# Gated delta rule and memory attention on Trainium2: every engine's queue order written out anew

## The reference, cut to what matters

```python
def gated_delta_rule(q, k, v, a, b, a_log, dt_bias):
    ...
    kk = jnp.einsum("bhnid,bhnjd->bhnij", kc, kc)
    lower = jnp.where(strict, bc[..., :, None] * kk * decay, 0.0)
    ...
    sol = lax.linalg.triangular_solve(lower + jnp.eye(CHUNK, dtype=f32), rhs, ...)
    p = jnp.einsum("bhnid,bhnjd->bhnij", qc, kc) * decay
    ...
    def step(state, xs):
        v_new = u_n - jnp.einsum("bhcd,bhde->bhce", w_n, state)
        o_n = jnp.einsum("bhcd,bhde->bhce", qg_n, state) + jnp.einsum("bhij,bhje->bhie", p_n, v_new)
        state = state * gl_n[..., None, None] + jnp.einsum("bhcd,bhce->bhde", kg_n, v_new)
        return state, o_n

def memory_attention(q_mem, mem_k, mem_v):
    s = jnp.einsum("bhtd,bhmd->bhtm", q, k).astype(jnp.float32) * MEM_DH ** -0.5
    p = jax.nn.softmax(s, axis=-1).astype(v.dtype)
    return merge_heads(jnp.einsum("bhtm,bhmd->bhtd", p, v))

y_mix, q_mem = gdn_branch(u @ gdn_w_in, ...)      # o = rms_norm(o, out_norm) * silu(z)
y_mem = memory_attention(q_mem, mem_k, mem_v)
y = jnp.concatenate([y_mix, y_mem], axis=-1) @ w_out
```

## Time and profile before

| | us |
|---|---|
| median of 3 runs | 2048.93 |
| lowest and highest | 2047.54, 2051.88 |
| the profiled execution's time | 2042.87 |
| its span | 2040.9 |
| TensorE busy in it | 1943.8 |
| VectorE busy | 1049.4 |
| ScalarE busy | 753.8 |

### The profile page before, as it was taken

How to read it: one execution, slowest core, us unless ns; L and a number is a source line. 1 busy time by engine, 2 the same in 40 slices (tenths; PEclk the granted TensorE clock), 3 DMA queues, 4 the chain that set the end, 5 groups by cost and what they waited for, 6 DMA issues and landing times.

```text
span 2040.9 us, 28553 instructions
## 1 busy us (share of the span) xinstructions
PE 1943.8 (95%) x11408; PEld 1692.7 (83%) x11408; DVE 1049.4 (51%) x1480; ACT 753.8 (37%) x1232; POOL 33.0 (2%) x31
## 2 busy tenths in 40 slices
PE   8999998999999997999999999999787999999997
PEld 8887788999999996888888777777686898888886
DVE  5644374664444458544444666676426253323335
ACT  5354342432232434423223425553445352212222
POOL 0100000100000000000000000000000000000000
PEclk9999999999999998999999999999778999999998
DMA  5211101233222332232223232222001223223221
GB/s 180 65 61 42 55 1 52 83 94 93 92 84 92 93 94 93 83 104 93 92 93 94 79 106 73 73 73 83 1 1 63 93 73 103 94 84 102 94 84 61
DMA packets 46607, 161.87 MB, mean 79 GB/s; under 512 B 4832, under 2 KB 7136, under 8 KB 46368
## 3 DMA queue, kind: packets, MB, share of 16 engines
q1 hardware_dynamic: 46208, 158.60, 24.5%
q10 hardware_dynamic: 288, 1.70, 0.2%
HBM read 156.09 MB, written 4.19 MB: 79 GB/s over the span
## 4 chain that ended last, share of the span: by engine, by line
PE 88%; DVE 6%; ACT 3%; DVEq 1%; issue 1%; DMA 0%; ACTq 0%; SPq 0%
PE ps L446 76%; PE ps L944 2%; PE ps L860 1%; DVE wlo L2126 1%; PE ps L964 1%; PE ps L833 1%; DVE W L2519 1%; PE ps L575 1%; PE ps L831 1%; PE ps L1107 1%; DVE AM L2305 1%; PE ps L1070 0%; PE ps L1104 0%; ACT RR L1960 0%; PE ps L1097 0%
## 5 line engine op out<-in xcount | busy, mean ns | idle before, releaser
L446 PE MATMUL ps<-UH,whi 128*128 128x264 f32 (+2 forms) x1920 | 655.1, 341 | 10.7 <-DVE wlo L2126 9.2
L446 PE MATMUL ps<-UL,whi 128*128 128x264 f32 (+2 forms) x1920 | 646.8, 337 | 0.0
L446 PE MATMUL ps<-UH,wlo 128*128 128x264 f32 (+3 forms) x1632 | 530.8, 325 | 0.0
L1351 ACT ACTIVATE whi<-raw 128x1024 fp32r<-128x1024 f32 x284 | 297.8, 1053 | 444.6 <-PE ps L446 424.8
L446 PEld LDWEIGHTS ps<-UH,whi 128*128 128x128 f32 x1920 | 365.0, 190 | 53.2 <-issue 12.6
L446 PEld LDWEIGHTS ps<-UL,whi 128*128 128x128 f32 x1920 | 364.7, 190 | 40.2 <-issue 2.4
L446 PEld LDWEIGHTS ps<-UH,wlo 128*128 128x128 f32 (+1 forms) x1632 | 309.6, 190 | 25.2
L2126 DVE TENSOR_TENSOR wlo<-raw,whi 128x1024 fp32r<-128x1024 f32 x248 | 308.1, 1245 | 39.7 <-ACT whi L1351 39.5
L446 PE MATMUL ps<-HH,whi 128*128 128x264 f32 (+1 forms) x768 | 246.4, 321 | 0.0
L446 PE MATMUL ps<-HL,whi 128*128 128x264 f32 (+1 forms) x768 | 246.3, 321 | 0.0
L446 PE MATMUL ps<-HH,wlo 128*128 128x264 f32 (+1 forms) x768 | 245.7, 320 | 0.0
(11 more groups left out here) (437 smaller groups left out, 2356.3 us busy)
## 6 DMA issues: line engine op xcount, KB each, us to landing
raw<-W SPq DMA_DIRECT2D x284, 512.0 KB, 3.5
H<-xT SPq DMA_DIRECT2D x4, 528.0 KB, 6.5
spill<-H SPq DMA_DIRECT2D x1, 2048.0 KB, 8.9
H<-spill SPq DMA_DIRECT2D x1, 2048.0 KB, 8.6
MEM<-memT ACTq DMA_DIRECT2D x1, 1024.0 KB, 4.7
out<-H SPq DMA_DIRECT2D x2, 512.0 KB, 2.9
out<-H SPq DMA_DIRECT2D x4, 256.0 KB, 3.1
masks<-masks SPq DMA_DIRECT2D x1, 768.0 KB, 9.9
```

The costliest lines, as they stand in the source:

```text
L446: mm = pe.matmul(dst, a, b, start=start and n == 0, stop=stop_ and n == 2)
L1351: act.activation(whi[s % NB][:, :, :], raw[s % NB][:, :, :], ACT.Copy).then_inc(w_hi, 1)
```

## The change

In the weights' layout, the levels' numbering, the memory map and the last projection tiles:

```diff
+    sizes[TILE0["wout2"]], sizes[TILE0["wout2"] + 1] = 16, 8
...
-LEVEL_ORDER = [(0, 32), (1, 32), (0, 64), (1, 64), (2, 32), (2, 64), (3, 32), (3, 64)]
+LEVEL_ORDER = [(0, 32), (0, 64), (1, 32), (2, 32), (1, 64), (2, 64), (3, 32), (3, 64)]
...
+        am_t, = region(scratch, ("am_t", [P, 2, SEQ], F32))
...
+        TXI, = region(S0 + 36 * SEQ * 4, ("TXI", [P, 32, 32], F32))
...
+                    if j == 34 and k in (2, 6):
+                        scores(k // 4)
...
             def scores(h):
+                b = 4 + 2 * (h % 2)
+                pe.wait_ge(*evacuated(TILE0["gin"] + 32 + h))
+                if h == 0:
+                    pe.wait_ge(N["l2_done"], 16)
+                    pe.wait_ge(G["dec"], 8)
+                if h >= 2:
+                    pe.wait_ge(N["ma_end"], h - 1)
...
+                    mm = pe.matmul(ps[:, b + c // 2, NMEM * (c % 2):NMEM * (c % 2 + 1)],
```

So the first 8 blocks of the output projection are now the memory heads' blocks of tiles 0 and 1, the next 16 the delta heads' blocks of tile 0 and of tile 1. The memory heads' products lie in PSUM banks 4 to 7 by the head's parity. TensorE's order (what was there before, with its loop over c, is removed):

```diff
                 b, p = 2 * (c % 2) if c < 2 else 0, c % 2
+                if c < 2:
+                    pe.wait_ge(G["pt"], 2 * c + 2)
+                else:
+                    pe.wait_ge(G["up"], levels_done(0 if c == 2 else 2, 64))
                 pe.wait_ge(G["base"], c + 1)
-                pe.wait_ge(G["inv"], 2)
...
+                turned(2 if c < 2 else 3, lambda x: YG[g][:, x, :]).then_inc(G["ot"], 1)
+
+            def memory_part(e):
+                t = TILE0["wout2"] + e
+                if e == 0:
+                    pe.wait_ge(N["om_hi"], HEADS)
+                    pe.wait_ge(N["om_lo"], HEADS)
+                for k in range(HEADS):
+                    wh, wl = take()
+                    passes(psum(t, SEQ), wh, wl, oh(k), ol(k), k == 0, False)
+
+            def heads_part(e):
+                t = st.tile
+                assert t == TILE0["wout2"] + e
+                for k in range(HEADS, 12):
+                    if k in (HEADS, 2 * HEADS):
+                        pe.wait_ge(G["lo"], 6 + k // HEADS)
+                    wh, wl = take()
+                    mm = passes(psum(t, SEQ), wh, wl, oh(k), ol(k), False, k == 11)
+                mm.then_inc(tile_done, 1)
+                st.tile += 1
...
-            for e in range(KT - 2):
-                tile(12, SEQ, oh, ol, before=mixed(e))
+            for j in range(36):
+                tile(KT, SEQ, u, ul, before=between(j))
+
+            pe.wait_ge(G["vtc"], 7)
+            queries(0, 1)
+            pe.wait_ge(*evacuated(TILE0["gin"] + 34))
+            queries(1, 0)
+            pe.wait_ge(G["vtc"], 8)
+            queries(2, 3)
+            shares_turned(0)
+            pe.wait_ge(*evacuated(TILE0["gin"] + 35))
+            queries(3, 2)
+            corner32(0)
+            memory_values(0)
+            shares_turned(1)
+            update32(0)
+            scores(2)
+            corner64(0)
+            memory_values(1)
+            corner32(1)
+            update64(0)
+            scores(3)
+            update32(1)
+            corner32(2)
+            shares_turned(2)
+            corner64(1)
+            memory_values(2)
+            update32(2)
+            shares_turned(3)
+            update64(1)
+            memory_values(3)
+            corner64(2)
+            pe.wait_ge(G["up"], levels_done(1, 64))
+            keys_turned(0, 2)
+            solved(0, 0)
+            keys_turned(1, 3)
+            solved(0, 1)
+            outer(0, 0)
+            update64(2)
+            within(0, 0)
+            state_keys(1, 0)
+            outer(0, 1)
+            corner32(3)
+            within(0, 1)
+            pe.wait_ge(G["kg"], 1)
+            keys_turned(2, 2)
+            state_keys(1, 1)
+            solved(1, 0)
+            state_queries(1, 0)
+            outer(1, 0)
+            update32(3)
+            pe.wait_ge(G["kg"], 2)
+            keys_turned(3, 3)
+            within(1, 0)
+            solved(1, 1)
+            state_queries(1, 1)
+            pe.wait_ge(G["kg"], 3)
+            outputs_turned(0, 0)
+            state_keys(2, 0)
+            pe.wait_ge(G["kg"], 4)
+            keys_turned(4, 3)
+            outer(1, 1)
+            within(1, 1)
+            state_queries(2, 0)
+            pe.wait_ge(G["kg"], 5)
+            queries(4, 3)
+            solved(2, 0)
+            pe.wait_ge(G["gt"], 1)
+            outputs_turned(0, 1)
+            state_keys(2, 1)
+            corner64(3)
+            pe.wait_ge(G["pt"], 5)
+            keys_turned(5, 3)
+            outer(2, 0)
+            within(2, 0)
+            state_queries(2, 1)
+            pe.wait_ge(G["gt"], 2)
+            outputs_turned(1, 0)
+            solved(2, 1)
+            pe.wait_ge(G["kg"], 6)
+            queries(5, 3)
+            update64(3)
+            state_keys(3, 0)
+            outer(2, 1)
+            pe.wait_ge(G["pt"], 6)
+            queries(6, 3)
+            within(2, 1)
+            state_queries(3, 0)
+            state_keys(3, 1)
+            pe.wait_ge(G["gt"], 3)
+            outputs_turned(1, 1)
+            solved(3, 0)
+            pe.wait_ge(G["pt"], 7)
+            queries(7, 3)
+            state_queries(3, 1)
+            solved(3, 1)
+            memory_part(0)
+            within(3, 0)
+            within(3, 1)
+            pe.wait_ge(G["pt"], 8)
+            outputs_turned(2, 0)
+            pe.wait_ge(G["gt"], 5)
+            outputs_turned(2, 1)
+            memory_part(1)
+            pe.wait_ge(G["gt"], 6)
+            outputs_turned(3, 0)
+            pe.wait_ge(G["gt"], 7)
+            outputs_turned(3, 1)
+            heads_part(0)
+            heads_part(1)
+            for e in range(2, KT - 2):
+                tile(12, SEQ, oh, ol)
```

ScalarE: the copies of the inverse in projection tile 34, squares into a region of their own, and the order:

```diff
+                if x == 10:
+                    act.wait_ge(G["inv"], 1)
+                    for q in range(4):
+                        a = 32 * q
+                        act.activation(WU[a:a + 32, :, a:a + 32], TXI[a:a + 32, :, :].rearrange("p t n -> p n t"), ACT.Copy)
...
+                    act.activation(squares[:, 4 * g + x, :], QS[g][:, x, :], ACT.Square, accum_out=SS[:, 4 * g + x:4 * g + x + 1])
...
+            wout2 = BLOCK0["wout2"] // SLOT
+            exps(0)
+            exps(1)
+            base(0)
+            shares_out(0)
+            base(1)
+            corner32(0)
+            memory_out(0)
+            shares_out(1)
+            exps(2)
+            corner64(0)
+            memory_out(1)
+            corner32(1)
+            base(2)
+            exps(3)
+            corner32(2)
+            shares_out(2)
+            corner64(1)
+            memory_out(2)
+            shares_out(3)
+            base(3)
+            memory_out(3)
+            keys_out(0, 2)
+            solved(0, 0)
+            corner64(2)
+            keys_out(1, 3)
+            solved(0, 1)
+            weights_hi(0, to=wout2 + 1)
+            for h in range(HEADS):
+                memory_hi(h)
+            rstd_heads(0, 0)
+            corner32(3)
+            keys_out(2, 2)
+            solved(1, 0)
+            queries_out(1, 0)
+            rstd_heads(0, 1)
+            weights_hi(0, to=wout2 + 2)
+            keys_out(3, 3)
+            rstd_heads(1, 0)
+            solved(1, 1)
+            queries_out(1, 1)
+            keys_out(4, 3)
+            gated_hi(0, 0)
+            rstd_heads(1, 1)
+            queries_out(2, 0)
+            solved(2, 0)
+            gated_hi(0, 1)
+            corner64(3)
+            keys_out(5, 3)
+            rstd_heads(2, 0)
+            queries_out(2, 1)
+            solved(2, 1)
+            gated_hi(1, 0)
+            queries_out(3, 0)
+            rstd_heads(2, 1)
+            gated_hi(1, 1)
+            solved(3, 0)
+            queries_out(3, 1)
+            solved(3, 1)
+            rstd_heads(3, 0)
+            gated_hi(2, 0)
+            rstd_heads(3, 1)
+            gated_hi(2, 1)
+            act.wait_ge(G["kv"], 6)
+            weights_hi(0, to=wout2 + 4)
             gated_hi(3, 0)
```

VectorE: the elimination's steps, the transposes, and the order; last the weights' layout on the host:

```diff
-            steps = (0, 2, 4, 6, 8, 11, 14, 17, 20, 23, 27, 31)
...
+            steps = (0, 3, 6, 9, 13, 17, 21, 25, 29, 31)
...
-                else:
+                elif x < len(steps):
                     eliminate(steps[x - 1], steps[x])
...
+                if x == 9:
+                    dve.drain()
+                    dve.transpose(TXI[:, :, :], XI[:, :, :]).then_inc(G["inv"], 1)
+                if x == 10:
+                    dve.transpose(TDG[:, :, :], XI[:, :, :].rearrange("p t s -> p s t")).then_inc(G["inv"], 1)
+                    top(0)
+                    top(1)
...
+            share(0)
+            queries(0, 1)
+            queries(1, 0)
+            share(1)
+            queries(2, 3)
+            queries(3, 2)
+            update32(0)
+            top(2)
+            share(2)
+            update64(0)
+            top(3)
+            update32(1)
+            share(3)
+            update32(2)
+            update64(1)
+            state(0, 0)
+            update64(2)
+            memory_lo(0)
+            output(0, 0)
             dve.drain()
```

(88 more changed lines are left out.)

237 lines of the change are left out of this document (39 added, 198 removed).

## The result

The changed kernel takes **1988.65 us** (median of 4 runs, 1986.23 to 1993.70) against 2048.23 (2047.35 to 2051.88) for the kernel before: ratio 0.9709, 95% interval 0.9684 to 0.9734. The forecast was 2004.7 with a range from 1990 to 2030: the direction was right, the size too small. Its profiled execution took 1990.95 us. The page of that profile answers to the earlier trace rows: the dip of slices 29 to 31 is gone.

The account below looks back on a forecast made before the run. TensorE bounds the kernel, with 35.1 us of waits and clock 0.81 in one stretch; 3.8 + 97.9 + 2 + 5 + 11.2 + 9.5 = 129.4 us against 173.6, gain 44.2, giving 2004.7 us, range 1990 to 2030.

Parts of the forecast that it names:

- part (7): TensorE's clock in the stretch: falls at narrow level-32 updates (5 us) and the idle end (4.5), 9.5 us, bounds 0 and 29.
- rival A: The clock stays full throughout, also at the end: 119.9 us, gain 53.7, 1995 us; chance 0.10.
- (4): New queue orders in the chain: the 35.1 us of waits shrink to 2 us up to the last chunk, bounds 0 and 10.
- (5): The chain's end: memory parts fill one wait, normalize, turn and gate remain, 5 us of TensorE idleness.
- The work: TensorE's products in the new chain, summed from unit prices at full clock: 97.9 us.
- Part (2): VectorE's elimination done by projection tile 33, four steps leaving 0.16 us idle in a tile: cost 0, bounds 0 and 2 us.
- Part (3): Beside tiles 34 and 35, four ScalarE copies of 2.0 us each, ending about 2 us before the chain begins.
- Part (1): Scores of heads 0 and 1 move into projection tile 34: 3.8 us there, winning only an earlier softmax start.
- B: The clock behaves as now though the waits are gone: 29 us in place of 9.5, gain 24.7, 2024 us; chance 0.17.
- C: The queues lock elsewhere and the 35.1 us of waits come back: gain 16, 2033 us; chance 0.11.
- D: The chain, now without rests, runs at 1.2 GHz all through: 222.8 us, loss 49, 2098 us; chance 0.05.
- E: Nothing moves, as the stretch is hidden; chance 0.02.

Follow-up runs that it names:

- e12: The changed kernel run again with nothing edited: 1988.99 us, ratio 0.9722.
- e1: The changed kernel with the level-32 updates of chunks 1 and 2 side by side, no work added: 2002.93 us, ratio 0.9775.
- e2: The changed kernel with chunk 0's level-32 update issued three times, its products left narrow: 2003.64 us, ratio 0.9773.
- e3: The changed kernel with chunk 0's level-32 update issued three times, its products widened to 128 columns: 1999.47 us, ratio 0.976.
- e4: The kernel before, order untouched, with the products of corners and level-32 updates widened to 128 columns: 2031.97 us, ratio 0.9914.
- e5: The changed kernel with the memory heads' products of output tiles 0 and 1 put back behind the last turned outputs: 1995.42 us, ratio 0.975.
- e6: The changed kernel with the scores of memory heads 0 and 1 put back behind the projection: 1992.79 us, ratio 0.9745.
- e10: The changed kernel with two neighbours swapped in ScalarE's and in VectorE's written-out orders: 1994.19 us, ratio 0.9753.
- e13: The two-swaps kernel (e10) run again with nothing edited, on one chip with the changed kernel: 1989.21 us, ratio 0.9721.

## Why the prediction was wrong, and what of it was right

In the terms of its sum, the stretch was forecast at 12.0 (tiles 34 and 35 as before) + 129.4 = 141.4 us, and measured at 129.3: 12.1 us too long.

**The step that failed is part (7), the clock.** It put 9.5 us on it: a fall by the narrow products in the four updates 32 (5), and the fall at the idle end (4.5). The profiled execution has 0.0, the clock is 1.00 throughout; e12 has 3.0, about half of it at each place. The mechanism was right. e1, e2 against e3, and e4 show that narrow products lower the clock of a busy TensorE, and in e12 the two places are the ones forecast: 1488 to 1492 directly behind the single update 32 of chunk 3, with no wait ahead, and 1533 to 1537 at the end. The size was wrong, because I took the price of the first fall from the earlier trace rows, where two updates stand in a row in the middle of other head products, and the fall lasts 11 us. Where one update stands alone the fall is under 4 us long, or doesn't come: in the changed kernel three narrow groups in a row, 5.30 us long, ran at 1.00. The 4.5 us for the end have no working, and the rows of before give less: half of the 1.85 us that TensorE is busy from 1571 to 1577.66, and (1 - 0.89) / 0.5 x 18.91 / 2 = 2.1 us behind, 3.0 together:

```profile
1571.00:1577.66 6.66, 1.85 (x9) 1.49 (x9) 4.06 (x6) 1.66 (x5) 0.00 (x0) 0.54 1.03 407
```

The lower bound of 0 was in the text; rival A (clock full, 119.9 us, or 131.9 with the tiles) had a chance of 0.10 and was the outcome.

**Idleness, parts (4) and (5)**: 2 + 5 us forecast, 5.0 measured (0.9 up to the last chunk, 4.1 at the end, against 1.5 + 1.9 + 1.6). The first place named as tight, the first corner behind the base blocks, is the 0.9 us wait; the others kept their slack. The longest wait is at the end, as forecast. e5 shows that the memory parts cover some of it.

**The work.** 97.9 us forecast for the chain, 97.48 busy from 1431.22 to 1533.72; scores in tile 34, 3.8 forecast, tiles 34 and 35 took 15.29 against 11.99, so 3.3. The heads' part of the output tiles took 11.50 against 11.2. This is 0.6 us too much forecast together, and 9.5 + 2.0 + 0.6 is the 12.1.

**Part (2)**, the elimination in ten tiles, at 0 us: right. From the evacuation of tile 28 to that of tile 33 it took 30.06 us before (1380.90 to 1410.96) and 30.06 after (1385.87 to 1415.93). VectorE waits for TensorE ahead of the evacuations of the fullest tiles, by as little as 0.17 us where 0.16 was forecast.

```profile
1385.87 0.69 DVE L2775 TENSOR_TENSOR ZQ<-ps,R 128x512 f32<-128x512 f32 x1 [0.65 <-PE ps L454]
1391.89 0.69 DVE L2775 TENSOR_TENSOR ZQ<-ps,R 128x512 f32<-128x512 f32 x1 [0.35 <-PE ps L454]
1397.89 0.69 DVE L2775 TENSOR_TENSOR ZQ<-ps,R 128x512 f32<-128x512 f32 x1 [0.17 <-PE ps L454]
```

**Part (3)**, four copies of 2.0 us each: right, 2.07, which end 1.5 us before the chain begins (2 forecast). ScalarE's timeline in tiles 34 and 35:

```profile
1421.38 8.30 ACT L1918 ACTIVATE WU<-TXI 32x1024 f32<-32x1024 f32 x4
1429.69 0.60 ACT L1899 ACTIVATE QKV<-ps 128x512 f32<-128x512 f32 x1
1430.32 0.48 ACT L1931 ACTIVATE am_p<-ps,am_s 128x256 f32<-128x256 f32 x1
```

**Part (1)** said that the early scores win nothing but an earlier softmax; e6 agrees: 0.8 us of waiting.

**The rest of the miss.** The median lies 16.1 us under the forecast: 12.1 of the stretch, 3.3 by which the medians' gain (59.6) exceeds the stretch's (56.3), and 0.7 of the median of before. The 3.3 aren't traced; behind the stretch the two profiled executions take the same time (444.3 and 443.9 us to the end of the span), so they presumably lie ahead of it, where executions spread. Against rival A's 1995.2 the outcome is 6.6 us lower: 2.6 in the stretch (131.9 to 129.3) and the same 3.3 and 0.7. The range left 5 us below A, which was too little for the spread between executions that this kernel shows.

**Rivals.** B (the clock as now): no, it is 1.00 and 0.97. Its 29 us were too many in any case: part of the low 59 us is idle, and the prediction's own sum of work gives 119.6 - 96.1 = 23.5. C (waits come back): no, 5.0 us. D (the chain at 1.2 GHz all through): no, 1.00. E: no. Two of the signs named failed: the stretch from the last projection tile on was to be about 126 us and was 114.0 (1431.22 to 1545.22), and the gain, 59.6 us, lies outside 34 to 52. The others held.

By the Trainium skill's rule the sum would have been 120 to 125 (132 to 137 with the tiles), nearer the outcome than mine, but for a wrong reason: by it e2 would have been as fast as e3, and e4 no faster than the kernel before.

What stays open: what decides between executions whether a single update, or the end, lowers the clock. The changed kernel and e12 are one program with the same waits, and yet differ in this. It also stays open how the 26.2 us of clock divide between the waits that went and the narrow products set apart: only the 12.9 us of e4 are shown to be the narrow products'.

## What to carry to other kernels

Where an engine must be in order and the stall list names several engines in turn, write the order out by the lateness of the data: the order gave 35 us here, and putting back the early inversion, on which two engines' work depends, cost 23. When a latency-bound chain has matmuls of few columns back to back, look at the granted clock with TensorE fully busy; if it is low, widen them, which cost nothing per record (0.11 us at 32, 64 and 128 columns) and gave 0.86% here, or set wide ones between. Price a clock fall by the work that stands around it. When an edit breaks up what lowers the clock, take seriously that the fall won't come at all. Check small differences against a second execution of the same kernel.

## What was not expected of the hardware

- A busy TensorE falls to the lower clock by narrow products alone: 0.53 over 11.00 us of 11.00 busy, 1.00 in the same window with 128 columns (e4). At full clock a record of these fp32 products (two records each) takes 0.11 us with 32, 64 or 128 columns.
- Idleness doesn't always lower it: at the changed kernel's end TensorE works only 3.77 of 7 us and the clock stays at 1.00. In e1, with the same waits there, it fell (6.31 busy of 7.00 us at 0.53).

```profile
1527.00:1534.00 7.00, 3.77 (x20) 2.83 (x19) 5.44 (x9) 5.24 (x16) 0.00 (x0) 1.00 1.01 393
```

- The same kernel's stretch, with the same waits, took 129.3 and 132.3 us in two executions, by the clock alone. Ahead of it, at tile 33, the profiled executions spread over 10.6 us (1409.46 to 1420.07), and those of one kernel, the two-swaps one, lie 7.9 us apart (1420.07 in e10, 1412.13 in e13).
